# A decoder layer on eight cores: score matmuls in groups of two steps, a new opening, and another plan of weight slots

## The reference, cut to what matters

```
mod = silu(c) @ w_ada + b_ada          # 9 x 1024: shift, scale and gate of three sub-layers
h = rmsnorm(x) * (1 + sc0) + sh0
x = x + 0.5 * g0 * ((silu(h @ w_gate) * (h @ w_up)) @ w_down)              # FFN 1, width 2816
h = rmsnorm(x) * (1 + sc1) + sh1
q, k, v, u, gv, gates = split(h @ w_in)
for each of 8 heads: two causal softmaxes (64 wide each) with a relative bias,
    attn = (p0 - lam * p1) @ v, then rmsnorm over the head's 128 channels   # causal, 2048 x 2048
y_a = attn @ w_a ; y_b = (gelu(u) * spatial(layernorm(gelu(gv)))) @ w_b
x = x + g1 * ((sigmoid(gate_a) * y_a + sigmoid(gate_b) * y_b) @ w_o)
h = rmsnorm(x) * (1 + sc2) + sh2
x = x + 0.5 * g2 * swiglu(h)                                                # FFN 2
```

## Time and profile before

| | |
|---|---|
| median of 3 runs | 1965.01 us (1964.53 to 1968.05) |
| the profiled execution | 1963.58 us |
| its span on the slowest core | 1962.0 us (the eight: 1954.7 to 1962.0) |
| PE busy | 1798.8 us, 92% |
| DVE, ACT, POOL busy | 1125.6, 746.8, 347.6 us |
| chain that ended last | PE 83%, DMA 6%, issue 4%, DVE 3%, ACT 3%, POOL 1% |
| weight loads (q0) / other loads and stores (q1) | 74.45 MB / 69.05 MB |

### The profile page before, as it was taken

The page is one execution under the profiler, slowest core; times in us unless marked ns, Lnnn a source line. Parts: engine busy times, 40 slices in busy tenths (PEclk is TensorE's granted clock), DMA queues, the critical chain, the costliest instruction groups (busy, mean ns, idle before and its releaser), DMA issues.

```text
span 1962.0 us, 35705 instructions; the slowest of 8 cores (1954.7 to 1962.0 us)
## 1 busy us (share of the span) xinstructions
PE 1798.8 (92%) x12410; PEld 962.0 (49%) x12580; DVE 1125.6 (57%) x2045; ACT 746.8 (38%) x1218; POOL 347.6 (18%) x430
## 2 busy tenths in 40 slices
PE   0679999999978999999999989989997999999998
PEld 0334444444435766766766644444443444444443
DVE  0566666666685465455445421696646766666666
ACT  0541111111164666666666669842218111111110
POOL 0000000000004544355445320471000000000000
PEclk9799999999989999999999999999998999999999
DMA  9815332223364102102103225138861111221104
GB/s 185 193 28 84 70 71 54 54 54 74 74 172 106 28 25 61 50 34 66 50 34 66 50 67 129 23 76 152 214 160 33 33 33 33 40 58 33 33 1 172
DMA packets 47966, 145.79 MB, mean 74 GB/s; under 512 B 5640, under 2 KB 6832, under 8 KB 40880
## 3 DMA queue, kind: packets, MB, share of 16 engines
q0 software_dynamic: 8928, 74.45, 21.0%
q1 hardware_dynamic: 38864, 69.05, 11.9%
HBM read 184.37 MB, written 33.56 MB: 111 GB/s over the span
## 4 chain that ended last, share of the span: by engine, by line
PE 83%; DMA 6%; issue 4%; DVE 3%; ACT 3%; POOL 1%; DVEq 0%; SPq 0%; ACTq 0%; POOLq 0%
PE psum L567 72%; PE psum L1138 6%; PE psum L1087 4%; DMA arena<-wblob 3%; DMA arena<-xT 2%; PE psum L1002 1%; ACT arena L1100 1%; ACT arena L736 1%; DVE arena L729 1%; PE psum L1185 0%; DVE arena L1378 0%; DVE arena L803 0%; DVE arena L1113 0%; POOL arena L1382 0%; ACT arena L692 0%
## 5 line engine op out<-in xcount | busy, mean ns | idle before, releaser
L567 PE MATMUL psum<-arena 128*128 128x512 bf16 (+4 forms) x8698 | 1546.4, 334 | 137.3 <-DVE arena L708 34.6
L567 PEld LDWEIGHTS psum<-arena 128*128 128x128 bf16 (+1 forms) x8868 | 772.8, 98 | 888.9 <-issue 193.0
L803 DVE SCALAR_TENSOR_TENSOR arena<-psum,arena 128x512 f32<-128x512 f32 x704 | 481.1, 743 | 29.0 <-PE psum L567 28.5
L779 ACT ACTIVATE arena<-psum 128x512 f32<-128x512 f32 x176 | 104.9, 597 | 753.2 <-PE psum L567 392.5
L1100 ACT ACTIVATE arena<-psum 128x1024 bf16<-128x1024 f32 (+1 forms) x288 | 273.1, 974 | 68.1 <-PE psum L1087 43.3
L782 DVE TENSOR_TENSOR arena<-arena,psum 128x512 bf16<-128x512 f32 x176 | 120.9, 688 | 308.4 <-PE psum L567 300.0
L192 POOL DMA_DIRECT2D arena<-wblob x62 | 33.9, 547 | 1118.7 <-PE psum L567 1021.6
L1138 PE MATMUL psum<-arena 128*128 128x129 bf16 x2176 | 172.8, 222 | 4.9 <-DVE arena L1157 2.5
L1138 PEld LDWEIGHTS psum<-arena 128*128 128x128 bf16 x2176 | 134.8, 99 | 40.2 <-issue 33.1
L1087 PE MATMUL psum<-arena 64*128 64x256 bf16 (+1 forms) x1152 | 106.8, 269 | 15.0 <-ACT arena L1100 9.3
L1113 DVE TENSOR_TENSOR arena<-arena 128x256 bf16<-128x256 bf16 (+1 forms) x184 | 75.1, 431 | 35.2 <-ACT arena L1100 13.1
(11 more groups left out here) (81 smaller groups left out, 788.5 us busy)
## 6 DMA issues: line engine op xcount, KB each, us to landing
arena<-wblob POOLq DMA_DIRECT2D x22, 1536.0 KB, 11.6
arena<-wblob POOLq DMA_DIRECT2D x32, 1024.0 KB, 10.0
zgate<-arena SPq DMA_DIRECT2D x64, 256.0 KB, 2.4
arena<-zgate SPq DMA_DIRECT2D x64, 256.0 KB, 10.4
arena<-xT SPq DMA_DIRECT2D x4, 2048.0 KB, 22.0
xspill<-arena SPq DMA_DIRECT2D x32, 256.0 KB, 4.6
arena<-xspill SPq DMA_DIRECT2D x8, 1024.0 KB, 18.2
outT<-arena SPq DMA_DIRECT2D x32, 256.0 KB, 2.2
```

The lines of the kernel that those rows point to most:

```text
L567: e.matmul(out_ap, l, r, start=s0, stop=s1),
L779: ta = B.op("act", lambda e, sap=sap, gb=gb: e.activation(sap[:], psum[:, gb, :], AF.Silu), deps=sdeps + [tg])
L803: tx = B.op("dve", lambda e, d=d, db=db, tsl=tsl: e.scalar_tensor_tensor(xT[:, d, tsl], psum[:, db, :], hg[:, d:d + 1], xT[:, d, tsl], ALU ...
```

## The change

1. `emit_S` takes a group of steps. In heads 0 to 6 it is given two steps, so that their eight score matmuls stand in one task that the planner cannot split, and the group is written ahead of the second product of the even step. Each step still has its own exponential. Head 7 goes step by step as before.
2. Gate units per head are [6, 6, 7, 7, 6, 6, 6, 12] instead of [4, 4, 8, 8, 8, 8, 6, 10].
3. Opening: each x block comes in two halves of 1 MiB with semaphores of their own. Conditioning slice 0 is tied to the first half of x block 0; slices 2, 1, 3 have no dependency; x block 1 waits for slice 3. FFN slice 0 comes in three parts of its own, the third tied to x block 1's first half. Slice 4 has no dependency; x block 2 waits for slice 4, slice 5 for x block 2's first half, x block 3 for slice 5, and FFN slice 1 for x block 3's first half. The shift and scale of channels 0 to 511 are finished apart from the others, and so is the gate.
4. Conditioning slices in FFN 1: two for each FFN slice (behind T = 1 and T = 3) from slice 1 on, one in slice 0, so that the last stands in slice 6. They all use slot 2, and the FFN slices alternate between slots 0 and 1. The slots of the att and gate slices are written out anew, and gate slice 3 comes behind att slice 7.

```diff
 def slice_plan():
-    order = [("ffn1", 0), ("ffn1", 1), ("ada", 6)]
-    nxt = 7
+    order = [("ffn1", 0), ("ffn1", 1), ("ada", 6), ("ada", 7)]
+    nxt = 8
     for g in range(2, NFG):
         order.append(("ffn1", g))
-        if nxt < 18:
-            order.append(("ada", nxt))
-            nxt += 1
...
+        for k in range(2):
+            if nxt < 18:
+                order.append(("ada", nxt))
+                nxt += 1
     order += [("att", 0), ("gate", 0), ("att", 1), ("att", 2), ("gate", 1), ("att", 3), ("att", 4), ("gate", 2), ("att", 5),
-              ("att", 6), ("gate", 3), ("att", 7)]
+              ("att", 6), ("att", 7), ("gate", 3)]
...
-        if key[0] in ("u", "gv"):
+        if key[0] == "ffn1":
+            slots[key] = key[1] % 2
+        elif key[0] == "ada":
+            slots[key] = 2
...
+        elif key[0] == "att":
+            slots[key] = (2, 0, 2, 1, 2, 0, 2, 0)[key[1]]
+        elif key[0] == "gate":
+            slots[key] = (1, 0, 1, 2)[key[1]]
...
+                if j == 0:
+                    W["load"][j] = [B.dma("pool", slots[k][:, q * 2048:(q + 1) * 2048], wb_d[:, offs[j] + q * 2048:offs[j] + (q + 1) * 2048],
+                                          s_w0[q], lead.get(("part", q), [])) for q in range(3)]
...
+        x_in(0)
+        ada_early(0, [x_tok[0][0]])
+        for i in (2, 1, 3):
+            ada_early(i)
+        x_in(1, [ada_load[3]])
+        lead[("part", 2)] = [x_tok[1][0]]
+        w_ensure(0)
+        ada_early(4)
+        x_in(2, [ada_load[4]])
+        ada_early(5, [x_tok[2][0]])
+        x_in(3, [ada_load[5]])
+        lead[1] = [x_tok[3][0]]
+        w_ensure(1)
+        lead[2] = [W["load"][1]]
...
                 if T == NT - 1:
                     w_release((name, g), w_rd[g])
-                    if ada_iter is not None:
-                        ada_iter(g)
+                if ada_iter is not None and T % 2 == 1 and (g, T) != (0, 1):
+                    ada_iter(g)
...
             if T == 0:
-                for i in range(4):
-                    ada_slice(i)
-                mod_finish0(0, None)
+                for k in range(2):
+                    ta_ = ada_slice(k)
+                    tb_ = ada_slice(k + 2)
+                    mod_finish0(k, (ta_, tb_))
...
-            ahead = [emit_S(steps[0]), emit_S(steps[1])]
+            ahead = emit_S(steps[0:2])
             later = []
             for i, step in enumerate(steps):
+                pair = step[0] < H - 1
+                if pair and i % 2 == 0:
+                    nx = steps[i + 2:i + 4]
+                    ahead += emit_S(nx) if nx[0][0] < H - 1 else emit_S(nx[0:1]) + emit_S(nx[1:2])
                 cur = ahead.pop(0)
                 toks = emit_PV(step, cur)
-                if i + 2 < len(steps):
-                    ahead.append(emit_S(steps[i + 2]))
+                if not pair and i + 2 < len(steps):
+                    ahead += emit_S(steps[i + 2:i + 3])
...
-        n_gate = [4, 4, 8, 8, 8, 8, 6, 10]
+        n_gate = [6, 6, 7, 7, 6, 6, 6, 12]
```

124 lines of the change are left out of this document (59 added, 65 removed).

## The result

The changed kernel took 1951.27 us (median of 4 runs, 1949.66 to 1952.77), the kernel before 1966.53 on the same chip: ratio 0.9924, 95% interval 0.9912 to 0.9936. It is faster by 0.76%, 15 us, where I had forecast 47. The time is above my range of 1898 to 1942. Rivals A (1930), B and D (1933) are too small as well, and C (1982) is far too large. Several terms failed at once.

The account below looks back on a forecast made before the run. PE, busy 1798.8 of 1962.0 us, was taken as the bound. Terms 12 + 1.5 + 7.5 + 3.2 + 12 + 11 = 47.2 us off 1963.6 gave 1916.4, as median 1918; range 1898 to 1942.

Parts of the forecast that it names:

- A: In attention: ACT sets the pace, so the paired scores save nothing; 1930 us, chance 0.17.
- B: Opening: gains nothing, x starved by queued weights, DVE's work not shrinking, first matmul up to 4 us later; 1933, chance 0.10.
- D: Planner puts fillers or scores elsewhere, waits return at two of the three places of weight waits; 1933 us, chance 0.07.
- C: Heads 0 to 6: PE stands at the unsplittable score group for the second exponential; slower, 1982 us, chance 0.06.
- The opening: Start of kernel: x block 3 lands near 84, block 2's gate and up matmuls start near 96; 11 us, bounds 4 and 17.
- Conditioning slices: Inside FFN 1: four PE waits for weights go, as slot 2 alone gives loads 21.6 us; 3.2 us, bounds -3 to 3.2.
- FFN 1 to attention: Between FFN 1 and attention: weight waits and clock drop go, early gate units fill idle PE; 12 us, ceiling 17.
- the planner can put them into the 8.1 us: Before attention: the eight first gate units (14 us of PE) fill PE's wait for DVE's residual additions and the norm.
- Scores in groups of two: Heads 0 to 6: 104 fewer group boundaries at 0.20 us each; 12 us taken, bounds 0 and 21.
- What could eat it: Heads 0 to 6: paired scores need both earlier exponentials; chain up to 3.5 us per pair against 3.73 of PE.
- Gates: Two gate units move from heads 0 to 6 into head 7's idle PE time; 1.5 us, between 0 and 3.5.
- The end of attention: Behind attention's last step: PE's 6.1 us wait for the u slice and slow matmuls go; 7.5 us, range 5 to 8.

## Why the prediction was wrong, step by step

**The opening (11 us forecast, 0 measured).** The transfers were nearly right: slice 0 issued at 33.6 (near 30), slice 5 at 64.8 (64), x block 3 there at 84.5 (84). Wrong was the step "They can now begin when those of block 1 are done, near 96": I took the arrival of x block 3 for what block 2 waited for. Block 2's own statistics are written behind unit (0,0)'s down products, so its squares ran at 96.0 with its x long there, and at 95.6 in the kernel before. That x block 3 landed there at 95.1 was a coincidence. A transfer that arrives early pays only if its first reader is not queued behind something else, and the row of that reader (squares, ten in a row, just ahead of the norm) stood in the trace before. My own test, "wrong if gate and up of block 2 start after 105", came out at 112.10.

**Conditioning slices (3.2, about 0).** The waits went as the step says; no weight wait is left in 125 to 555 us. But the earlier trace rows are core 0's. Cores 3, 4 and 6 of the kernel before waited 1.3 to 2.9 us in that stretch and cores 1, 2, 5 and 7 not at all, and the median core's time from mm500 to S0, which also holds what follows FFN 1, is 415.8 us before and 415.5 after. The four cores with such waits were the four slowest (1960.4 to 1962.0 us, the others 1954.7 to 1956.6), so their waits may well have counted. After the change the four slowest are cores 0, 2, 4 and 6, those on which ACT waits longest for the stores. I had put the profiled core's wait into the sum in full and not asked what another core would then have.

**FFN 1 to attention (12, 0).** Two steps failed. The weight waits of 6.5 us were 2.4 on core 1 and 2.4 to 6.5 over the cores, the same error as above. And "the planner can put them into the 8.1 us" was right and harmful. I had named what would be late next ("the x spill and the last norm, on which the head 0 chain on POOL depends") and then priced the filling as a gain. The planner put gate units ahead of FFN 1's last down matmuls, so the last norm got its input 4.6 us later (580.3 instead of 575.7), with five store buffers as well. Each gate unit also needs a copy, all eight of them on ACT in the changed kernel, in order, ahead of the last norm; with three store buffers four cores stood for a store besides. In all the last norm's exponential came at 597.0 instead of 588.8, and PE then stood 8 us for head 0's chain on POOL. Held units gave 4.9 us at S0, five buffers 1.3, and a slower queue for the stores took 3.6.

**Scores in groups of two (12, 7.8 alone and 1.3 beside the rest).** The price of a boundary was right by the rows (0.55 to a score group, 0.47 to a transpose; eight scores 0.54). Their number was 222 before, not 230, as 30 groups of eight stood there already and not 22, so 96 went and not 104, and 19 us was the ceiling. PE's busy time in heads 0 to 6, median of the cores, fell from 472.1 to 458.8 us with the pairs alone, 13.3 us, at a granted clock of 0.99 instead of 1.00. PE on core 1 was busy for 447.1 of 470 us with the pairs alone and did more matmuls in it than before. These are the windows of 625 to 1095 us on core 1, before, pairs alone, and after:

```profile
625.00:1095.00 470.00, 451.80 (x5294) 326.73 (x5292) 238.11 (x628) 307.73 (x552) 227.60 (x287) 1.00 0.19 46
```

```profile
625.00:1095.00 470.00, 447.07 (x5430) 340.25 (x5428) 253.36 (x649) 312.50 (x565) 234.62 (x293) 1.00 0.19 47
```

```profile
625.00:1095.00 470.00, 441.45 (x5325) 336.45 (x5326) 254.70 (x648) 300.82 (x544) 230.22 (x289) 0.99 0.20 48
```

Failed is "What could eat it: the group of steps i + 2 and i + 3 needs all four score banks, so both exponentials before it". That wait vanished (0.5 us), though my sign for rival A, heads 0 to 6 taking 490 us again, came out. (The handover that I had assumed at 0.2 us is 0.11 in the trace before: the score row that starts at 865.41 is 0.39 long, and its exponential starts at 865.91.) What ate it stands on the other side of PE: products now come two steps together, the next query block's product meets accumulators that DVE (L1180) has not yet read, and the transposes meet POOL. I had looked only at what the scores wait for, not at who must empty a bank for the products that move with them. Alone these waits were 8.6 and 3.7 us, and 8.0 and 3.9 with the old gate numbers beside all other edits (median of the cores), but 12.8 and 6.4 in the changed kernel. So the new gate numbers, which I had treated apart, took some 7 us of what the pairs gave. What the 12 us of waits that the pairs bring by themselves hang on stays open: ordering at the turns brought 3.9 us without held gates and 1.1 with them.

The Trainium skill (TensorEngine Tiling (Array Packing), PSUM Bottleneck) says that once packing speeds TensorE up, the evacuation of PSUM may bound. I had tied it to ACT and the score banks. The runs agree with it as far as the waits for L1180 go (2.3 to 12.7 us), at the product's banks and on DVE.

**Gates (1.5, about 6 without the pairs).** I costed only a shift of work into idle time. But the numbers also set when a gate slice's slot comes free: beside the new slots the old ones cost 2.4 to 6.5 us of weight waits in heads 0 to 6, the new ones none. With 12 units in head 7, PE's waits there for exponentials fell from 3.9 to 1.1 us on core 1 (plan alone against all but the pairs), and head 7 is 3.9 us shorter; heads 0 to 6 are 2.1 shorter. The old numbers in the changed kernel cost 10.7, of which head 7 has 4.6; in heads 0 to 6 the weight waits and the waits at the accumulators cancelled.

**The end of attention (7.5, 6.2 and 5.5 more).** The wait went. Behind it core 1 takes 784.1 us from the last product to the end instead of 789.4 from the first u matmul, 3.1 of it in PE's busy time. Part of that is the clock, for the matmuls behind the wait no longer run slow (granted clock 0.77 to 0.86 on the eight cores in 1155 to 1175 us before, 1.00 on all after). I had 1.7 for that; what the rest of the 5.5 us is stays open.

**The rivals.** None had the mechanism in full. D came nearest: the planner put fillers elsewhere, and where the weight waits of the earlier trace rows had been, 8 us of waiting for POOL stood. But it priced this at 15 us of 32. A had nearly the right size for its term, by the wrong engine. B's time was near the truth of its own term (gain of nothing) by luck: neither was x starved nor the first matmul later (61.8 before, 61.1 after).

In all, the sum had 47.2 and the measured terms make -0.8 + 2.2 + 2.3 + 6.2 + 5.5. Of the 32 us missed, 27 were promised ahead of the first scores. There I had added savings on four places without asking, once for the whole stretch, what would be last when all had gone; it was a norm at both ends of FFN 1, held by its place behind other work.

## A version that beats both

The changed kernel with held gates ran at 1941.16 (0.9887 of before, 0.9862 to 0.9913); with turns and earlier norms besides, 1940.07 and 1941.35 on two other chips (0.9844 and 0.9855, with intervals of 0.7 to 0.8% to each side). By the profiled moments the latter is 2 to 5 us ahead at the end, and its own two executions are 3.2 apart; its time can't be told from the former's.

## What to carry to other kernels

For a transfer or a weight wait that goes, find the first reader and ask which instruction stands ahead of it on its engine; if that is the written order, the earlier arrival is worth nothing until the order changes too. Filler for an idle TensorE is not free when it can run ahead of the last matmuls that the critical chain waits for, or when each piece needs a copy on an engine of that chain: start it only when the chain's last step is out. When units of filler are moved, ask what slot their weights hold and which load waits for it. When groups are fused, list every bank that the moved instructions write and who empties it, not only those of the fused operation; and before a wait goes into a sum, look for it on every core, since the slowest core may be another one after the change.

## What the runs showed of the hardware

- Cores of one execution are 7.3 us apart before, 9.8 after and 16.0 with the pairs alone, with different waits for the same weights: 6.5 us on core 0 and 2.4 on core 1 at one place.
- A store of 256 KB issued by POOL beside other traffic lands later than by SP: the median of the eight stores between 565 and 600 us is 3.1 to 5.7 us from issue to landing by SP and 6.5 to 8.7 by POOL, core for core, and ACT's waits for them rose from 4.6 to 11.5 us on core 4.
- Groups of eight score matmuls and the next product start 0.55 us apart (879.18 to 879.73 in the changed kernel), near the 0.54 worked out from the earlier trace rows, and the products ahead of them take 0.55 as before.

```profile
878.63 0.62 PE L1161 MATMUL psum<-arena 128*128 128x129 bf16 x8
879.18 0.61 PE L1103 MATMUL psum<-arena 64*128 64x256 bf16 x8
879.73 0.63 PE L1161 MATMUL psum<-arena 128*128 128x129 bf16 x8
```
